# A three-tap convolution and its gate move from VectorE to GpSimd in a two-block transformer kernel

## The reference, cut to what matters

```python
(a_b, a_c, a_x, b_u, c_q, c_k, c_v,
 d_q, d_k, d_v, d_f, gate_logits) = _split(u @ w_in[l], IN_SPLITS)
y_a = short_conv_mixer(a_b, a_c, a_x, a_conv_w[l], a_w_out[l])
...
def short_conv_mixer(gate_b, gate_c, xin, conv_w, w_out):
    return (gate_b * causal_depthwise_conv(gate_c * xin, conv_w)) @ w_out
```

## Time and profile before

| | before |
|---|---|
| median of three runs | 1765.37 us (1762.72 to 1768.25) |
| the profiled execution, its own time | 1769.86 us |
| its span | 1768.1 us |
| TensorE busy | 1690.8 us (96%) |
| VectorE busy | 1093.3 us (62%) |
| ScalarE busy | 802.0 us (45%) |
| GpSimd busy | 36.8 us (2%) |
| TensorE's granted clock, mean | 0.985 of full speed |

### The profile page before, as it was taken

How to read it: one execution, slowest core, us unless ns; L and a number is a source line. 1 busy time by engine, 2 the same in 40 slices (tenths; PEclk the granted TensorE clock), 3 DMA queues, 4 the chain that set the end, 5 groups by cost and what they waited for, 6 DMA issues and landing times.

```text
span 1768.1 us, 25871 instructions
## 1 busy us (share of the span) xinstructions
PE 1690.8 (96%) x11028; PEld 1522.2 (86%) x11028; DVE 1093.3 (62%) x1275; ACT 802.0 (45%) x1057; POOL 36.8 (2%) x60
## 2 busy tenths in 40 slices
PE   6999999999999999999999989999999999889987
PEld 6999899877889999899989987788999988679866
DVE  4454678787665544654467888776654466655654
ACT  5343544454445333534354455444443355544552
POOL 0000000000000000000000000000000001000000
PEclk9999999999999999999999999999999999899989
DMA  7555455434546555555556444354655442215120
GB/s 276 188 191 189 168 215 177 158 143 143 176 161 219 185 188 191 198 181 178 189 175 223 175 156 151 131 183 167 214 191 183 180 178 87 96 43 198 65 94 24
DMA packets 49106, 292.96 MB, mean 166 GB/s; under 512 B 5456, under 2 KB 5856, under 8 KB 21344
## 3 DMA queue, kind: packets, MB, share of 16 engines
q1 hardware_dynamic: 45504, 278.94, 44.4%
q10 hardware_dynamic: 3488, 12.38, 2.1%
HBM read 290.23 MB, written 1.06 MB: 165 GB/s over the span
## 4 chain that ended last, share of the span: by engine, by line
PE 71%; DVE 12%; ACT 7%; issue 4%; DVEq 4%; DMA 1%; POOL 1%; ACTq 0%; SPq 0%; POOLq 0%
PE ps L1511 21%; PE ps L1513 21%; PE ps L1512 21%; DVE wlo L977 4%; ACT whi L630 3%; DVEq L1264 2%; DVE mix L1173 1%; DVEq L1178 1%; ACT prob L839 1%; PE ps L1971 1%; PE ps L1654 1%; DMA raw<-stream 1%; PE ps L1609 1%; PE ps L1655 1%; DVE small L1265 1%
## 5 line engine op out<-in xcount | busy, mean ns | idle before, releaser
L977 DVE TENSOR_TENSOR wlo<-raw,whi 128x2048 fp32r<-128x2048 f32 (+2 forms) x270 | 603.5, 2242 | 402.7 <-ACT whi L630 395.4
L1511 PE MATMUL ps<-xhi,whi 128*128 128x256 f32 (+1 forms) x2000 | 570.9, 285 | 0.9 <-ACT mix L898 0.9
L1513 PE MATMUL ps<-xhi,wlo 128*128 128x256 f32 (+1 forms) x2000 | 567.2, 284 | 0.0
L1512 PE MATMUL ps<-xlo,whi 128*128 128x256 f32 (+1 forms) x2000 | 567.1, 284 | 0.0
L630 ACT ACTIVATE whi<-raw 128x2048 fp32r<-128x2048 f32 (+2 forms) x270 | 498.4, 1867 | 13.0 <-DMA raw<-stream 12.0
L1511 PEld LDWEIGHTS ps<-xhi,whi 128*128 128x128 f32 (+1 forms) x2000 | 383.4, 192 | 5.3 <-issue 2.2
L1512 PEld LDWEIGHTS ps<-xlo,whi 128*128 128x128 f32 (+1 forms) x2000 | 383.4, 192 | 2.6
L1513 PEld LDWEIGHTS ps<-xhi,wlo 128*128 128x128 f32 (+1 forms) x2000 | 383.3, 192 | 0.5
L1511 PE MATMUL ps<-whi,yar 128*128 128x512 f32 x620 | 248.7, 401 | 14.6 <-ACT mix L892 7.6
L1512 PE MATMUL ps<-wlo,yar 128*128 128x512 f32 x620 | 243.5, 393 | 0.0
L1513 PE MATMUL ps<-whi,yar 128*128 128x512 f32 x620 | 243.3, 392 | 0.0
(11 more groups left out here) (200 smaller groups left out, 1374.1 us busy)
## 6 DMA issues: line engine op xcount, KB each, us to landing
raw<-stream SPq DMA_DIRECT2D x214, 1024.0 KB, 4.8
raw<-stream SPq DMA_DIRECT2D x80, 512.0 KB, 4.4
raw<-stream SPq DMA_DIRECT2D x10, 768.0 KB, 4.3
gpre<-pre_gain ACTq DMA_DIRECT2D x9, 512.0 KB, 4.6
gpost<-post_gain ACTq DMA_DIRECT2D x6, 512.0 KB, 5.8
mix<-cum ACTq DMA_DIRECT2D x2, 1024.0 KB, 4.6
raw<-stream SPq DMA_DIRECT2D x2, 640.0 KB, 3.9
h<-x_in SPq DMA_DIRECT2D x2, 512.0 KB, 6.1
```

The lines of the kernel that those rows point to most:

```text
L977: TT(wlo[:, s, 0:w], raw[:, s, 0:w], whi[:, s, 0:w].bitcast(F32), ALU.subtract).then_inc(lo_v, 1)
L1511: pe.matmul(dst, lh, rh, start=first, stop=False)
L1512: pe.matmul(dst, lh, rl, start=False, stop=False)
L1513: return pe.matmul(dst, ll, rh, start=False, stop=last)
```

## The change

The steps `a_conv` leave VectorE's program and go to GpSimd's. One instruction now serves all four channel groups: the weight of a tap is spread over 256 columns as an operand that repeats itself, and product and addition are two instructions of 1024 columns instead of one that does both. The product of taps 1 and 2 goes to `thb`. GpSimd waits for chunk 7 before tap 0, and for chunk 9 before the product with `a_b`. VectorE, which now reads `acc_a` in `a_split` without having written it, waits for `mixa_done` there. Nothing else changes; the order of steps is the same.

```diff
@@ gpsimd
                     elif kind == "o_norm":
                         rsqrt(l * 8 + 3, step[1], 4, step[1])
+                    elif kind == "a_conv":
+                        tap = step[1]
+                        if tap == 0:
+                            cols_taken(pool, l, 7)
+                        w = pr1("a_conv").rearrange("p (m k) -> p m k", m=KH)[:, :, tap:tap + 1].to_broadcast([P, KH, T])
+                        part = thb[:, :].rearrange("p (m t) -> p m t", m=KH)
+                        pool.tensor_tensor(part if tap else acc_a, pad_a[:, :, tap:tap + T], w, ALU.mult)
+                        if tap:
+                            pool.drain()
+                            pool.tensor_tensor(acc_a, acc_a, part, ALU.add)
+                        pool.drain()
+                        if tap == A_CONV - 1:
+                            cols_taken(pool, l, 9)
+                            pool.tensor_tensor(acc_a, acc_a, a_b, ALU.mult).then_inc(mixa_done, 1)
@@ vector
-                    elif kind == "a_conv":
-                        tap = step[1]
-                        for m in range(KH):
-                            w = pr1("a_conv")[:, m * A_CONV + tap:m * A_CONV + tap + 1]
-                            v = pad_a[:, m, tap:tap + T]
-                            if tap == 0:
-                                TS(acc_a[:, m, :], v, w, None, ALU.mult)
-                            else:
-                                STT(out=acc_a[:, m, :], in0=v, scalar=w, in1=acc_a[:, m, :], op0=ALU.mult, op1=ALU.add)
-                        dve.drain()
-                        if tap == A_CONV - 1:
-                            cols_taken(dve, l, 9)
-                            TT(acc_a, acc_a, a_b, ALU.mult).then_inc(mixa_done, 1)
                     elif kind == "a_split":
+                        dve.wait_ge(mixa_done, l + 1)
                         dve.wait_ge(ahi_done, l + 1)
                         TT(ylo[0], acc_a, yhi[0].bitcast(F32), ALU.subtract).then_inc(ya_ready, 1)
```

## The result

The changed kernel takes 1770.99 us (median of 20 runs, 1767.28 to 1774.16), the kernel before 1763.97 (20 runs, 1759.86 to 1769.79). The ratio is 1.0036, with a 95% interval from 1.0027 to 1.0045: slower by 6.3 us, 4.8 to 7.9 (the two medians differ by 7.0). Forecast were 9.2 us more. The two profiled executions are nearer to each other (spans of 1768.1 and 1769.3 us), because that of before was one of its long ones; so the traces are compared within the mixers, and the times by the ratio.

A forecast was written before the change was run, and what follows sets the result against it. VectorE was taken to bound the mixers from 283 to 409 us. GpSimd's 13.8 us of blocking less 9.2 of room gave 4.6 us a layer, 9.2 in two, added to the 1765.37 median: 1774.6 us, range 1763 to 1781.

The forecast's parts named there:

- Where the kernel is bound, and that the freed time is worth 0.7 us: Mixers, 283 to 409 us: VectorE is on the chain; its removed work gains only 0.4 us a layer, 0.7 in two.
- What a GpSimd instruction costs: Each of six 128x1024 GpSimd instructions a layer: 2.3 us taken, bounds 1.22 and 2.8; 13.8 us for six.
- The page's figure: Skill's 4497 ns for a 2048-column two-input addition on GpSimd; half is 2.25 us, six would be 13.5 us.
- VectorE stands still while GpSimd reads: From 273 to 309 us, VectorE instructions with two SBUF inputs are blocked by GpSimd instructions that read SBUF.
- All of GpSimd's time falls on VectorE: First mixer: GpSimd blocks VectorE for 13.8 us; less 9.2 us of room, it is 4.6 us late a layer.
- the room of 9.2: VectorE, 272.9 to 309.3 us: holes of 1.99 and 2.55 plus 1.75 and 2.89 removed can absorb 9.2 us.
- The walk between 273 and 299: VectorE, taking turns with GpSimd: about 4 us late at 285.93, 7 at the next split, 4 to 5 from 298.79.
- TensorE's wait for the low half: Low half ends about 301.3, TensorE wants it at 300.8: half a microsecond, left out of the sum.
- TensorE is not on the chain from 311 to 409, so the clock adds nothing: From 311.5 to 409.2 us more 1.2 GHz pieces may come, but TensorE is off the chain: nothing added.
- (a): Rival: VectorE is not blocked by GpSimd, or its instructions take near 1.2 us; 0.7 us gained, 1764.7; chance 0.30.
- (b): Rival: the freed 4.64 us a layer of taps and gate reaches the end; 9.3 us gained, 1756.1; chance 0.08.
- (c): Rival: GpSimd starves, its gate ends about 305 to 308 and ScalarE waits; about 1773.5 us; chance 0.12.

The follow-up runs named there:

- e1: Changed kernel without the short convolution and its gate on either engine, the waits kept; ratio to the kernel before 0.9992.
- e2: Changed kernel with 15 GpSimd memsets of 1024 columns in place of its six instructions, convolution and gate left out; ratio to the kernel before 0.9979.
- e3: Changed kernel with 11 one-input GpSimd copies of 1024 columns in place of its six instructions, convolution and gate left out; ratio to the kernel before 0.9982.
- e8: Changed kernel with each GpSimd product made as four of 256 columns with a scalar per partition; ratio to the kernel before 1.0037.
- e9: Changed kernel with GpSimd's first tap waiting for chunk 10 instead of chunk 7; ratio to the kernel before 1.0100.
- e6: Changed kernel with each of the three products of a layer made twice on GpSimd; ratio to the kernel before 1.0077.
- e11: Changed kernel with the three products on ScalarE as twelve copies, additions and gate on GpSimd in pieces of 256 columns; ratio to the kernel before 1.0020.
- e4: Changed kernel with the same GpSimd instructions spread in time: tap 1 waits for chunk 8, tap 2 for 9, gate for 10; ratio to the kernel before 1.0033.
- e7: Kernel before with the change's wide form (spread weights, 1024 columns), but on VectorE at the old place; ratio to the kernel before 1.0034.
- e5: Changed kernel with each of GpSimd's six instructions cut into four of 256 columns, drains kept; ratio to the kernel before 0.9998.
- e10: Kernel before with only tap 2 in the wide form on VectorE; ratio to the kernel before 1.0010.

## Why the prediction was right, and where its sizes were off

- *Where the kernel is bound, and that the freed time is worth 0.7 us.* Right: e1 shows 0.33 us a layer at the scores, for 0.36 computed. The time of e1 (0.9992) agrees; e2 and e3 are 3 to 4 us under before, which is more, and their traces differ from e1's in nothing before the fifth group. I have no cause for that; the clock is a suspect, as the mean granted clock of e2's executions goes from 0.988 (at 1765.47 us) to 0.994 (at 1757.13).
- *What a GpSimd instruction costs.* 2.3 taken; measured 1.90 for a product with spread weights and 2.40 for an addition or the gate, 12.9 us for six instead of 13.8.
- *The page's figure.* The estimate of 2.25 us from the Trainium skill (GPSIMD Engine Reference, 3.1 Elementwise — side-by-side cycle accounting) lies between the two measured values, and 13.5 against 12.9 for the sum.
- *VectorE stands still while GpSimd reads.* Shown: in after by VectorE's rows, by e2 to be the reading and not the activity, by e3 to need one input only. The Trainium skill (SBUF — State Buffer, Who interferes with whom) said this for any GpSimd instruction that reads SBUF, and the traces agree: 2.29 us became 4.03 beside products, 3.15 beside copies, and stayed 2.29 beside memsets. They agree less well in e8, where products with a scalar per partition, which read SBUF too, cost VectorE 0.28 us in four.
- *All of GpSimd's time falls on VectorE.* The term that was mis-sized: 13.8 predicted, 11.2 measured (11.2 in the second layer too: 4.04, 9.26 and 4.33 us). 0.9 of the difference is the shorter instructions, and 1.7 that each holds VectorE for 0.3 us less than it lasts. Less the room of 9.2 this leaves 2.0, and 2.28 and 1.91 were measured, for 4.6. The room itself was right: e3 puts 7.8 us into it without a trace left. e9 takes its first half of 4.5 us away and comes to the scores 4.3 and 4.6 us later than after. By VectorE's rows of the first layer, the stretching plus the idle time that is left, less the 9.0 us of idle time in e1, gives the distance to e1's scores within 0.5 us in after and in every one of e3 to e6, e8, e9 and e11 (2.2 for 2.6 in after, 6.7 for 6.9 in e9).
- *The walk between 273 and 299.* VectorE was to be 4 us late at 285.93, 7 at the next split and 4 to 5 from 298.79 on; it was 6.9, 5.1 and 2.2, as turns go by instruction, VectorE's first went to short ones, and nothing of GpSimd's was left after 288. TensorE's wait for the low half was put at 0.5 us at most and was 1.47 and 1.10. e4 shows that this has no price of its own.
- *TensorE is not on the chain from 311 to 409, so the clock adds nothing.* The step that failed. It was read rightly from the chain before, but the lateness puts TensorE on it: one more stretch at 1.2 GHz after the first transposes takes the first layer from 2.28 to 3.32 us, and e7 from 1.71 to 4.18. This error and the mis-sized blocking have opposite signs: 2 x 2.1 us expected by the corrected sum, 5.6 us by the fifth group (3.32 + 2.25), 6.3 in time, 9.2 predicted. That the forecast is no further off is in part luck.
- *The rivals.* (a), no blocking, is refuted by VectorE's rows; (b) by e1; (c), a starving GpSimd, by its own rows: only one instruction of six waited, 1.86 us, and the gate was done at 288.25, ten microseconds ahead of its date.

## What to carry to other kernels

Moving elementwise work from a VectorE that is on the path to an idle GpSimd is not free parallelism when both read SBUF: take the time of GpSimd's instructions that read SBUF, without its own waits, and count it against VectorE's holes at that place, and only against those that are still to come when GpSimd can start. If it must be done, cut GpSimd's instructions small (e5: no loss, against 6 us) and, which no run here tried, order VectorE's work so that its turns beside GpSimd go to long instructions and not to short ones. And where lateness makes TensorE wait, look at the granted clock of the next ten microseconds before calling that engine out of the chain.

## What was not expected of the hardware

- Turns between the engines went by instruction: with GpSimd's 1024 columns back to back, four VectorE products of 0.48 us took 9.26 us together.
- A GpSimd instruction held VectorE for some 0.3 us less than it lasts alone: 11.2 us for 12.9 in after, 7.8 for eleven copies of 1.05 in e3, 0.35 for a piece of 0.61 in e5. GpSimd's busy time in the profile is no measure of it, as it contains GpSimd's own waits (28.7 us a layer in e5).
- On GpSimd the spread weight is cheaper than the scalar: 1.90 us for a product of 4 x 256 columns with the weight repeated over the columns, 0.92 for one product of 256 with a scalar per partition, and so an estimated 3.7 for four (6.0 to 7.3 with the waits for splits).
- The same wait of TensorE at the first transposes, 1.63 us in both layers of after, was followed by a stretch at 1.2 GHz in one and not in the other. In e5, with 1.30 us, the granted clock stayed at 1.00; in e10, with 1.92, it went to 0.83 over ten microseconds. How late VectorE is does not decide it: e6, 6.73 and 6.34 us late with waits of 1.44 and 1.59, has no such stretch, and e10, 0.83 late, has.
